# Attention scores as three products of rounded parts: the scores of the pairs with a difference, the factor on POOL, and the chunk ends a tile later

## The reference, cut to what matters

```
s = jnp.einsum('bqhcd,bshcd->bhcqs', qb, k).astype(jnp.float32) * scale + bias[None, :, None]
p = jax.nn.softmax(s, axis=-1)
attn = p[:, :, 0] - lam * p[:, :, 1]
return jnp.einsum('bhqs,bshv->bqhv', attn.astype(v.dtype), v)
```

## Time and profile before

| | us |
|---|---|
| median of 3 runs | 2124.36 |
| lowest, highest | 2124.08, 2124.7 |
| profiled execution | 2126.04 |
| its span (first to last instruction) | 2124.2 |
| PE busy in the span | 2109.9 |
| DVE, ACT, POOL busy | 1127.6, 818.2, 873.1 |
| granted clock of PE, mean | 0.998 |

### The profile page before, as it was taken

The page is one execution under the profiler, slowest core; times in us unless marked ns, Lnnn a source line. Parts: engine busy times, 40 slices in busy tenths (PEclk is TensorE's granted clock), DMA queues, the critical chain, the costliest instruction groups (busy, mean ns, idle before and its releaser), DMA issues.

```text
span 2124.2 us, 33781 instructions
## 1 busy us (share of the span) xinstructions
PE 2109.9 (99%) x13386; PEld 1804.1 (85%) x13386; DVE 1127.6 (53%) x1701; ACT 818.2 (39%) x1362; POOL 873.1 (41%) x379
## 2 busy tenths in 40 slices
PE   9999999999999999999999999999999999999998
PEld 9987899999999777888888788888887788888887
DVE  6678766525632476420333579566774644543125
ACT  5258544223323584421333323344433432322224
POOL 3313434434444554444444433243444444444442
PEclk9999999999999999999999999999999999999999
DMA  6610245343434403333333465233233233333331
GB/s 178 168 56 2 56 140 144 90 120 103 137 90 134 133 2 92 97 95 94 92 96 94 134 130 153 79 86 86 86 88 95 87 112 89 99 89 92 89 101 66
DMA packets 375411, 210.77 MB, mean 99 GB/s; under 512 B 26659, under 2 KB 367876, under 8 KB 374392
## 3 DMA queue, kind: packets, MB, share of 16 engines
q1 hardware_dynamic: 364974, 192.61, 31.8%
q10 hardware_dynamic: 10314, 16.41, 2.8%
HBM read 196.97 MB, written 15.40 MB: 100 GB/s over the span
## 4 chain that ended last, share of the span: by engine, by line
PE 59%; issue 27%; POOL 12%; DVE 0%; ACT 0%; DMA 0%; POOLq 0%; SPq 0%; DVEq 0%; ACTq 0%
PE acc L1097 15%; PE acc L1098 15%; PE acc L1099 15%; POOL w_lo L919 12%; PE acc L1185 3%; PE ops L1254 2%; PE tps L1194 1%; PE acc L979 1%; PE ops L1248 1%; PE acc L980 1%; PE acc L981 1%; PE tps L1157 1%; DMA xin<-in_x 0%; PE ops L1409 0%; SPq L740 0%
## 5 line engine op out<-in xcount | busy, mean ns | idle before, releaser
L919 POOL TENSOR_TENSOR w_lo<-raw,w_hi 128x1024 fp32r<-128x1024 f32 x326 | 800.1, 2454 | 1126.5 <-ACT w_hi L1731 1116.0
L1731 ACT ACTIVATE w_hi<-raw 128x1024 fp32r<-128x1024 f32 x325 | 344.5, 1060 | 1005.5 <-PE acc L1099 985.7
L1097 PE MATMUL acc<-hr_hi,w_hi 128*128 128x512 f32 x1056 | 421.4, 399 | 0.1
L1099 PE MATMUL acc<-hr_hi,w_lo 128*128 128x512 f32 x1056 | 417.7, 396 | 0.0
L1098 PE MATMUL acc<-hr_lo,w_hi 128*128 128x512 f32 x1056 | 417.6, 395 | 0.0
L1097 PE MATMUL acc<-hn_hi,w_hi 128*128 128x264 f32 (+1 forms) x840 | 246.7, 294 | 0.0
L1099 PE MATMUL acc<-hn_hi,w_lo 128*128 128x264 f32 (+1 forms) x840 | 244.2, 291 | 0.0
L1098 PE MATMUL acc<-hn_lo,w_hi 128*128 128x264 f32 (+1 forms) x840 | 244.2, 291 | 0.0
L1097 PEld LDWEIGHTS acc<-hr_hi,w_hi 128*128 128x128 f32 x1056 | 198.5, 188 | 48.6 <-issue 1.1
L1099 PEld LDWEIGHTS acc<-hr_hi,w_lo 128*128 128x128 f32 x1056 | 198.4, 188 | 47.9
L1098 PEld LDWEIGHTS acc<-hr_lo,w_hi 128*128 128x128 f32 x1056 | 198.5, 188 | 47.3 <-issue 0.7
(11 more groups left out here) (486 smaller groups left out, 3755.6 us busy)
## 6 DMA issues: line engine op xcount, KB each, us to landing
raw<-in_w_up SPq DMA_DIRECT2D x64, 512.0 KB, 4.0
raw<-in_w_down SPq DMA_DIRECT2D x64, 512.0 KB, 3.9
raw<-in_w_in SPq DMA_DIRECT2D x56, 512.0 KB, 3.8
raw<-in_w_ffn_gate SPq DMA_DIRECT2D x22, 512.0 KB, 3.7
raw<-in_w_ffn_up SPq DMA_DIRECT2D x22, 512.0 KB, 3.8
raw<-in_w_in_even SPq DMA_DIRECT2D x18, 512.0 KB, 7.1
raw<-in_w_ffn_down SPq DMA_DIRECT2D x16, 512.0 KB, 3.8
raw<-in_w_in_odd SPq DMA_DIRECT2D x10, 512.0 KB, 5.4
```

The source lines that it names most:

```text
L919: nc.gpsimd.tensor_tensor(w_lo[:, part], raw[:, slot], w_hi[:, part].bitcast(F32), ALU.subtract).then_inc(sems["lo"], T.up("lo"))
L1097: mm(out, w_hi[:, part, w0 + k, :], xh, start=s0, stop=False)
L1099: ins = mm(out, w_lo[:, part, w0 + k, :], xh, start=False, stop=s1)
L1731: fn(w_hi[:, n % 2], raw[:, n % 4], ACT.Copy).then_inc(sems["hi"], T.up("hi"))
```

## The change

There are four edits. (1) The scores of the 16 A pairs (not of `A_METAS`) are no longer four fp32 products of `qkv_e`, but twelve fp32r products: for each half of the keys and each of the two softmaxes, hi x hi, hi x lo and lo x hi. ACT rounds the eight tiles of queries and keys (`round_tile`), seven of them in the last seven tiles of `even_in` and the eighth in step 5 of `attend`. POOL forms the rests (`rest_of`): four during the last tiles of `even_in`, the others between its first factors, in steps 1, 2, 3 and 6. The parts lie in the space of `mix_e_hi` and `mix_e_lo`, which is written only later. (2) The factor -lam x sum / sum of an A pair, a [128 x 1] operation, goes from DVE to POOL (`factors`); DVE raises `inverse` behind the reciprocal and waits for `factor`. (3) In the steps whose pair s-1 has a difference, DVE does `outputs(s-5)` no longer ahead of `tops(s)` but behind it and behind the reciprocal, so between reciprocal and the difference. (4) `chunk_ends` on PE, `keep_ends` on DVE and the bank counts on ACT go from tile (1, 0) to tile (1, 1), and the scan steps are spread anew.

```diff
+                p.products = [(o, slice(0, P), c, HALF, q_parts[a][64 * o:64 * o + 64, P * t:P * t + P],
+                               k_parts[b][64 * o:64 * o + 64, c:c + HALF], n == 0, n == 2)
+                              for c in (0, HALF) for n, (a, b) in enumerate(((0, 0), (0, 1), (1, 0))) for o in range(2)]
+                p.split = 2 * hd + 2
...
+            def factors(pairs):
+                for s, p in enumerate(pairs):
+                    T.saw("inverse")
+                    pool.wait_ge(sems["inverse"], T.at("inverse"))
+                    st = stat[0:p.nq, (s + LAG) % RING]
+                    nc.gpsimd.tensor_scalar(st[:, 6:7], p.den(st, 0), lam_neg[0:p.nq], st[:, 5:6], ALU.mult,
+                                            ALU.mult).then_inc(sems["factor"], T.up("factor"))
+                    if s < len(later):
+                        later[s]()
+
+            def rest_of(x):
+                T.saw("a_hi")
+                pool.wait_ge(sems["a_hi"], T.at("a_hi"))
+                nc.gpsimd.tensor_tensor(A_LO[x], qkv_e[:, x, :], A_HI[x].bitcast(F32), ALU.subtract).then_inc(
+                    sems["a_lo"], T.up("a_lo"))
+            later = [lambda x=x: rest_of(x) for x in A_TILES[4:7]] + [lambda: None] * 2 + [lambda: rest_of(7)]
...
@@ PE, scores(s)
+                    if p.split:
+                        pe.wait_ge(sems["a_lo"], p.split)
@@ PE, middle_after
-                    if (n, x) == (1, 0):
+                    if (n, x) == (1, 1):
                         chunk_ends()
@@ ACT
+            def round_tile(x):
+                fn(A_HI[x], qkv_e[:, x, :], ACT.Copy).then_inc(sems["a_hi"], T.up("a_hi"))
...
+                if m >= 10:
+                    stored(b)
+                    round_tile(even_in.order[m])
@@ DVE, shares(s) of a pair with a difference
-                    step(v.reciprocal(st[:, 5:6], p.den(st, 1)))
-                    step(v.scalar_tensor_tensor(st[:, 6:7], st[:, 5:6], lam_neg[0:p.nq], p.den(st, 0), ALU.mult, ALU.mult))
+                    T.saw("factor")
+                    dve.wait_ge(sems["factor"], T.at("factor"))
@@ DVE, attend
-                    if 0 <= s - LAG - 1 < n:
+                    second = 0 < s <= n and pairs[s - 1].differ
+                    if 0 <= s - LAG - 1 < n and not second:
                         outputs(s - LAG - 1)
...
+                    if second:
+                        inverse(s - 1)
+                        if s > LAG:
+                            outputs(s - LAG - 1)
                     if not rooted and 0 <= s - 1 < n:
                         shares(s - 1)
@@ DVE, middle_tile
-                    if 1 <= n <= 4 and (n, x) != (1, 0):
-                        for _ in range(((0, 8, 8), (4, 7, 7), (9, 10, 10), (7, 4, 4))[n - 1][x]):
+                    if 1 <= n <= 4 and (n, x) > (1, 1):
+                        for _ in range(((0, 0, 9), (6, 9, 9), (9, 10, 10), (9, 7, 4))[n - 1][x]):
                             next(scanning, None)
```

More of the change, by code:

```diff
@@ L487, in transposed_blocks_program @@
             "gate", "gated", "mixed_hi", "mixed_lo",
-            "negmax", "exp", "recip", "eps_rows", "scaled", "probs", "p_full", "p_stored", "metas",
+            "a_hi", "a_lo", "negmax", "exp", "inverse", "factor", "recip", "eps_rows", "scaled", "probs", "p_full", "p_stored", "metas",
             "dve", "act",
@@ L552, in transposed_blocks_program @@
             joint = False
+            split = 0
             def turned_metas(self, bank):
@@ L595, in transposed_blocks_program @@
         out_a = qkv_e[:, 8:12, :].rearrange("p a b -> p (a b)")[:, 0:16 * P].rearrange("p (n d) -> p n d", d=P)
+        A_TILES = even_in.order[10:17] + [7]
+        A_HI = {x: mix_e_lo[:, 1 + n, :] for n, x in enumerate(A_TILES[0:7])}
+        A_LO = {x: mix_e_hi[:, n, :] for n, x in enumerate(A_TILES[0:7])}
+        A_HI[7], A_LO[7] = mix_e_hi[:, 7, :], mix_e_lo[:, 0, :]
         A_PAIRS = []
@@ L601, in transposed_blocks_program @@
                 c0 = 384 - P * t
+                q_parts, k_parts = ([x[n] for x in (A_HI, A_LO)] for n in (hd, 4 + hd))
+                p.products = [(o, slice(0, P), c, HALF, q_parts[a][64 * o:64 * o + 64, P * t:P * t + P],
+                               k_parts[b][64 * o:64 * o + 64, c:c + HALF], n == 0, n == 2)
+                              for c in (0, HALF) for n, (a, b) in enumerate(((0, 0), (0, 1), (1, 0))) for o in range(2)]
+                p.split = 2 * hd + 2
                 p.differ = True
@@ L943, in normalise @@
                         sems["scaled"], T.up("scaled"))
+            def factors(pairs):
[13 more added lines that the diff above has]
+            later = [lambda x=x: rest_of(x) for x in A_TILES[4:7]] + [lambda: None] * 2 + [lambda: rest_of(7)]
             before_even_out = even_in.count + even_last.count + 1
             before_odd_out = sum(x.count for x in order[:order.index(odd_out)]) + 1
-            lows(0, before_even_out)
+            lows(0, before_even_out - 3)
+            T.saw("roped")
+            pool.wait_ge(sems["roped"], T.at("roped"))
+            for n, tiles in zip(range(before_even_out - 3, before_even_out), (A_TILES[0:1], A_TILES[1:3], A_TILES[3:4])):
+                low(n % 4, n % 2)
+                for x in tiles:
+                    rest_of(x)
+            factors(A_PAIRS)
             normalise(B_PAIRS, len(A_PAIRS))
@@ L1847, in swap_keys, with attend @@
                 dma(to[64:128], k[0:64], "kswap_in")
-            def attend(pairs, metaT):
+            def attend(pairs, metaT, last_tile=None):
                 n, last_square, ring_0 = len(pairs), None, T.ring["o_"]
@@ L1901, in attend @@
                         copies(s - LAG)
+                    if last_tile and s == LAG + 1:
+                        last_tile()
                     if rooted and s > last_square + 3 and s - 2 < n:
@@ L1998, in token_stats, with round_last @@
                 T.saw("rstd")
+            def round_tile(x):
+                fn(A_HI[x], qkv_e[:, x, :], ACT.Copy).then_inc(sems["a_hi"], T.up("a_hi"))
+            def round_last():
+                for kind in ("t_stored0", "t_stored1"):
+                    act.wait_ge(sems[kind], T.at(kind))
+                round_tile(7)
             def even_duty(m, s, t, b):
@@ L2062, in _ @@
             T.saw("swap_ready", 2)
-            attend(A_PAIRS + B_PAIRS, metaT_e)
+            attend(A_PAIRS + B_PAIRS, metaT_e, round_last)
             residual(even_out, 16, False)
@@ L2299, in middle_tile @@
                             group_exponentials(n - 1)
-                        if n == 1:
-                            for _ in range(2):
-                                others(T, "t_")
-                                others(T, "o_")
+                    if (n, x) == (1, 1):
+                        for _ in range(2):
+                            others(T, "t_")
+                            others(T, "o_")
                     if x == 1:
@@ L2573, in tops, with inverse @@
                             sems["s_stored"], T.up("s_stored"))
-                def shares(s):
+                def inverse(s):
                     p = pairs[s]
@@ L2579, in shares @@
                     dve.wait_ge(sems["exp"], T.at("exp"))
+                    v.reciprocal(st[:, 5:6], p.den(st, 1)).then_inc(sems["inverse"], T.up("inverse"))
+                def shares(s):
+                    p = pairs[s]
+                    st = stat[0:p.nq, (s + LAG) % RING]
                     if not p.differ:
+                        T.saw("exp", 2)
+                        dve.wait_ge(sems["exp"], T.at("exp"))
                         v.reciprocal(st[:, 4:6], st[:, 2:4]).then_inc(sems["recip"], T.up("recip"))
@@ L3412, in middle_tile @@
                         group_tops(n - 1)
-                        if n == 1:
-                            keep_ends()
+                    if (n, x) == (1, 1):
+                        keep_ends()
                     if x == 2 and n:
```

## The result

The changed kernel took 2158.62 us in the median of 5 executions (2156.33 to 2159.89), the kernel before 2124.36 (2124.08 to 2124.79). The ratio is 1.0159, with an interval of 1.0146 to 1.0172: 34 us slower, where 20 slower was forecast and 31 was the upper end of the range. A second set of four executions (run 11) took 2154.81 (2153.88 to 2156.2). So its own time moves by 6 us over nine executions; runs 11 and 12 show a part of the reason.

A forecast was written before the change was run, and what follows sets the result against it. Three limits were taken to tie at 2.71 us a step: PE's stream, DVE's stream and the score-accumulator loop. Terms +20.0 + 1.4 - 1.6 = +19.8 us on the 2124.36 median gave 2144 us, range 2137 to 2155.

The forecast's parts named there:

- The chain: Attention: values wait for the copy behind the tops, so steps take 4.19 us, not 2.71, 13 times; +20.0 us with corrections.
- the old lengthening: Meta pair's copies in attention: 1.19 us in place of 0.28, which lengthened a step before as well, so counted as 0.
- One sign of the prediction: Profile after, attention: PE idle about 1.1 to 1.3 us a step before the values matmuls, released by DVE's copy.
- New scores: A pairs' scores on PE: 12 fp32r products run side by side, 0.75 us of PE's stream, 0.90 to last end.
- the rival with 1.28 to 1.44 us: A pairs' scores on PE take the full 1.28 to 1.44 us, giving 2150 to 2152 us; chance 0.09.
- Factor: A pairs' factor on POOL: 0.2 us, plus 0.1 us for each of two hops, mostly covered by the copy.
- Rests: First attention steps: POOL's rests hold up differences of steps 1, 2 and 3; +1.4 us net; step 6 costs 0.
- the 1.2 us for shorter scores and factors: First attention steps: 1.2 us saved by shorter scores and factors, set against the rests' hold-ups.
- Rival D: Attention: PE's clock falls to 1.2 GHz, values and scores 2.2 us longer in 13 steps, +29, 2173 us; chance 0.05.
- POOL's set-up: Before the first factor: bounds 0 and 52 us, taken as 0; rival that it is paid once, +5.5 us, chance 0.10.
- Chunk ends: Middle stage: a tile later, PE's 1.65 us hole before them goes; bounds -1.65 and 0, taken as -1.6 us.
- about 1 us to spare: Middle stage: slack claimed for DVE's rotation of queries and keys, which a group's scores need and which could be late next.

The follow-up runs named there:

- run 11: The changed kernel itself measured once more, nothing altered, four executions: 2154.81 us, ratio 1.0144.
- run 12: The changed kernel with eight products of ones added on PE in its idle time ahead of step 4: 2155.27 us, ratio 1.0146.
- run 1: The kernel before with only the A pairs' output copy moved behind the tops and the reciprocal: 2147.1 us, ratio 1.0103.
- run 3: The changed kernel with the output copy put back ahead of the tops: 2138.71 us, ratio 1.006.
- run 2: The changed kernel with PE's wait for an A pair's bank moved to just before that pair's own values: 2136.64 us, ratio 1.0055.
- run 8: The changed kernel with the bank wait at the values, rests behind the difference, and chunk ends and scan steps as before: 2123.64 us, ratio 0.9998.
- run 4: The kernel before with only the chunk ends a tile later and the scan steps spread anew: 2131.66 us, ratio 1.0034.
- run 7: The kernel before with the chunk ends a tile later, but the scan begun in the same tile behind their copies: 2124.77 us, ratio 1.0001.
- run 5: The changed kernel with the bank wait at the values, and POOL's rests held until the difference ends: 2130.8 us, ratio 1.003.
- run 6: The kernel before with chunk ends in their old place and only the scan steps spread as in the changed kernel: 2132.71 us, ratio 1.0037.
- run 9: The changed kernel with only the meta pair's copies put back ahead of the tops: 2151.68 us, ratio 1.0129.

## Why the prediction was wrong

*The chain (forecast +20.0): right, in mechanism and size.* The wait was in front of the values matmuls, on DVE's copy, 13 times. Without a fall of the clock behind it, step 5 to step 18 took 56.8 us (run 11), forecast 57. Inside, two errors cancel. The steady step is 4.12 and not 4.19 (the copy follows 0.07 us behind the start of the reciprocal, not 0.19), which is -0.9 in 13 steps. And the meta pair is under-counted by 0.9. Before, its values on PE (2.31 us in place of 1.31) and its copies on DVE (1.19 in place of 0.28) ran side by side, and step 17 was 1.03 us longer than the period for both. In the chain they stand one behind the other: steps 17 and 18 take 5.28 and 5.17 us. The prediction set the copies against the old lengthening and had no term for the values. Run 1 gives the same loss from this edit alone. One sign of the prediction did not follow from its own sum: it named 1.1 to 1.3 us of idle time on PE a step, where 4.19 less 2.46 is 1.73; the trace has 1.51.

*New scores:* forecast 0.75 us of PE's stream and 0.90 to the end, measured 0.83 and 1.00. Pairs do run side by side, and the rival with 1.28 to 1.44 us is out. By the Trainium skill ("TensorE: Matmul & The Clock Gate", "LDWEIGHTS (loading the stationary operand)") a load takes its columns over 1.2 GHz, an estimated 1.28 us for 12 loads of 128 columns one behind the other; the trace has all 12 products within 0.83 us.

*Factor:* taken at 0.2, measured 0.34; the whole detour 0.63 us. In the changed kernel the copy lies inside it; in run 3, where the copy is elsewhere, it lengthens the period.

*Rests (forecast +1.4), a term of the right kind and too small:* a difference of 0.77 us lasts 1.8 beside a rest, at steps 1, 2, 3 and 6. The one at step 6 cost nothing, as forecast, behind the long chain (in run 2, without the chain, it cost 1.0). Step 5 came 1.9 us late with the clock kept up (run 12), 2.4 in run 11 and 3.05 in the first profile. In run 8, without the hold-ups, it came 1.25 early, as the 1.2 us for shorter scores and factors said. So the hold-ups cost 3.15 us, where 2.6 was taken, and the clock 0.5 to 1.15 more. What I did not see is that the hold opens a gap of over 2 us on PE at the change from fill to attention, and that PE comes out of it at the lower clock.

*Rival D, the clock,* was put as one fall over all 13 steps, +29 us, at 0.05. It did not fall in the steady chain, with 1.5 us of waiting in 4.1. In the attention it fell behind the two longest waits, at a price of 0.5 to 1.15 us at the first and 1.4 at the second, and not in every execution. That accounts for the 24.0 us in the first profile against 21.9 in run 11. It is part of the spread of the kernel's own time; that it is all of it is not shown.

*POOL's set-up* is not paid: the first factor took 0.34 us like the others, 0.27 us behind the start of the reciprocal that released it and 0.4 us behind the instruction of set-up (129.6 and 129.99 us). The 6 us that the Trainium skill gives for a first call ("GPSIMD Engine Reference", "Instruction dispatch") are not seen here.

*Chunk ends (forecast -1.6, bounds -1.65 and 0): the step that failed.* Measured +7.1 alone (run 4), +5.8 in the profile. The prediction said that DVE had "done as many or fewer scan steps than before at every tile up to (3, 2)" and took this as harmless. It is the harm, in two steps. The idle 5.2 us in tile (1, 1) are work that must be made up, and it is made up ahead of rotations that PE waits for: measured against POOL's subtraction, the first of them starts 1.1 us later in run 4 than in run 7. And so it falls behind this subtraction instead of ahead of it, which holds it up for 2.1 us (3.30 us in place of 1.21); most of the wait is this second step. The prediction had no term for it, though it had one for the same hold-up at the rests. The first step could have been read from the profile of the kernel before: in these two stretches of it, with the scan in both, DVE is busy 97% of the time (the third number, 9.73 and 9.77 of 10 us), though over the whole kernel it is busy 53%.

```profile
1270.00:1280.00 10.00, 10.00 (x46) 8.17 (x45) 9.73 (x23) 3.52 (x10) 1.76 (x2) 1.00 0.25 63
1280.00:1290.00 10.00, 10.00 (x54) 8.37 (x53) 9.77 (x11) 2.80 (x4) 4.78 (x2) 1.00 1.07 310
```

Part of this busy time is itself a hold-up by POOL: the scan step at 1284.23 us lasts 2.54 us, where others of its line last 0.4. The "about 1 us to spare" that I gave to the rotations had no row; in the trace of the kernel before it is 0.78 us at the rotation in question. The gain was over-read as well: 1.65 us was the wait of one execution, which lay 1.7 us above the median of its kernel.

*The sum:* chain 18.2 to 22.6 (runs 1, 2 and 11), spread of the scan 7.1 (run 4), rests with the clock 5.8 (runs 2 and 5), all else -0.6 (run 8). These add to 30.5 to 34.9 us, against 30.3 to 34.3 in the two sets. The agreement is in part built in, since the 18.2 and the 5.8 are differences between these very runs; what is independent is run 1 (22.6) and run 4 (7.1), each on the kernel before. The kernel lies 11 to 15 us above the forecast. Of these 7 to 9 are the chunk ends; the rest is the first steps and the falls of the clock.

*What stays open:* when a wait of some 2 us brings the clock down and when not (run 11 waited 2.40 us and kept it), and how much of the 6 us between the two sets of the changed kernel is the clock of the attention, how much that of the middle stage, and how much lies elsewhere; none of its longest executions was profiled.

## What to carry to other kernels

When work is moved back on an engine, look for waits that stand earlier than they need: this one was taken two operations ahead of its use, cost nothing for as long as the copy came first, and made 20 us of loss when it came second. Where an engine gives up its share of a background job for one tile, look at how full it is in that stretch and not in the kernel; fewer steps done early means more to do under a deadline. Where an operation on two SBUF tiles moves in time, look at which work of POOL it will then lie beside. And a hole read from one execution is an upper bound until a second profile shows it.

## What the runs showed of the hardware that I had not expected

- The clock fell from 2.4 to 1.2 GHz in or behind waits of 2.14 to 2.16 us (five profiles of five, at 136 or at 138 us), of 2.40 us (the first profile, runs 1 and 12, but not run 11) and of 2.71 us (the first profile and runs 2, 3, 6 and 9, but not runs 4, 5, 11 and 12), and never in the 12 steps with waits of 1.4 to 1.5 us in 4.1 to 5.3. Eight products of ones in the first wait kept it up.
- A POOL subtraction of 528 columns from SBUF holds up a DVE scalar_tensor_tensor on two SBUF inputs (1.8 us in place of 0.77); one of 1024 columns holds up a DVE tensor_tensor on two SBUF inputs (3.30 us in place of 1.21). Neither effect shows at the tops beside a rest, whose one input is in PSUM (0.70 us).
- Twelve fp32r products on alternating halves of the rows take 0.12 us a pair, 0.23 for the first pair.
